# Sixteen of 24 modulation products computed on GpSimd instead of TensorE, in a one-core two-block transformer kernel

## What is computed

```python
c_act = jax.nn.silu(c)
mod = (c_act @ w_ada[l] + b_ada[l])[:, None, :]                  # block 1: 1024 x 6144
sh1, sc1, ga1, sh2, sc2, ga2 = jnp.split(mod, 6, axis=-1)
h = rmsnorm(x, ln1_pre[l]) * (1.0 + sc1) + sh1
proj = h @ w_in[l]                                               # 1024 x 2816
...                                                              # window attention, chunked recurrence (hgrn2)
mix = jnp.concatenate([attn, hg], axis=-1) @ w_out[l]
x = x + ga1 * rmsnorm(mix, ln1_post[l])
...                                                              # 32 experts, then block 2:
mod = (jax.nn.silu(c) @ w_ada + b_ada)[:, None, :]               # 1024 x 6144
mod_ctx = jax.nn.silu(c_ctx) @ w_ada[:, :2 * d] + b_ada[:2 * d]  # the first third, for a second vector
```

## Time and profile before

| | us |
|---|---|
| median of 3 runs | 2185.94 |
| lowest, highest | 2184.53, 2190.42 |
| the profiled execution | 2187.34 |
| its span, first to last instruction | 2185.5 |
| mean granted TensorE clock, of full speed | 0.938 |

### The profile page before, as it was taken

One profiled execution on the slowest core, in us unless ns is written; L12 is line 12 of the kernel. 1 busy time (PEld: TensorE's weight loads), 2 busy tenths in 40 slices (PEclk: granted clock), 3 DMA queues, 4 the chain that ended last, 5 costly groups with the idle time before them and its releaser, 6 DMA issues.

```text
span 2185.5 us, 32417 instructions
## 1 busy us (share of the span) xinstructions
PE 1910.1 (87%) x13222; PEld 1296.8 (59%) x13223; DVE 858.6 (39%) x1997; ACT 551.9 (25%) x1026; POOL 475.8 (22%) x523
## 2 busy tenths in 40 slices
PE   5999998759878279899999989899999999999766
PEld 3777787635433168678766657645565555556432
DVE  3154534353221422521477432334444534443226
ACT  4242512311101431412477412201111211111111
POOL 1000000023221100000345000004444544454320
PEclk9998999879999689979999999889999999999998
DMA  8665521359999451211477322348999999999977
GB/s 323 238 244 178 208 117 58 144 195 413 417 418 397 158 141 53 87 23 55 110 147 168 79 105 88 124 174 340 384 405 358 409 407 376 383 381 399 358 281 307
DMA packets 102472, 527.33 MB, mean 241 GB/s; under 512 B 28002, under 2 KB 28306, under 8 KB 48172
## 3 DMA queue, kind: packets, MB, share of 16 engines
q1 hardware_dynamic: 63216, 451.70, 52.3%
q0 software_dynamic: 36256, 64.54, 10.8%
q10 hardware_dynamic: 2844, 8.85, 1.2%
HBM read 519.36 MB, written 51.90 MB: 261 GB/s over the span
## 4 chain that ended last, share of the span: by engine, by line
PE 71%; DMA 16%; DVE 7%; ACT 3%; issue 2%; SPq 0%; POOL 0%; ACTq 0%; POOLq 0%; DVEq 0%
PE ps L251 31%; PE ps L1738 16%; DMA arena<-in_egu 11%; PE ps L1812 8%; DMA arena<-in_ada 3%; PE ps L1704 2%; PE ps L411 2%; PE ps L2942 1%; PE ps L1799 1%; PE ps L433 1%; PE ps L2968 1%; PE ps L2254 1%; DMA arena<-in_bs_row 1%; PE ps L1073 1%; DMA arena<-y_rows 1%
## 5 line engine op out<-in xcount | busy, mean ns | idle before, releaser
L1738 PE MATMUL ps<-arena 128*64 128x256 f32 x4096 | 484.1, 391 | 63.6 <-DMA arena<-in_egu 52.3
L1738 PEld LDWEIGHTS ps<-arena 128*64 128x64 f32 x4096 | 300.2, 141 | 272.0 <-issue 75.8
L251 PE MATMUL ps<-arena 128*128 128x256 f32 (+4 forms) x1268 | 325.3, 418 | 3.3 <-ACT arena L3092 0.9
L251 PEld LDWEIGHTS ps<-arena 128*128 128x128 f32 (+1 forms) x1268 | 228.0, 204 | 84.1 <-issue 63.6
L1686 POOL DMA_INDIRECT arena<-h_rows,arena x160 | 192.2, 1201 | 297.4 <-DVE arena L1667 133.4
L1692 POOL DMA_INDIRECT y_rows<-arena x160 | 160.5, 1003 | 404.7 <-DVE arena L1843 347.2
L1812 PE MATMUL ps<-arena 128*64 128x512 f32 x1024 | 242.2, 602 | 6.5 <-DVE arena L1807 2.5
L1807 DVE COPY arena<-ps 128x256 f32<-128x256 f32 (+1 forms) x96 | 36.5, 380 | 432.8 <-PE ps L1799 432.8
L1786 ACT ACTIVATE arena<-ps 128x256 f32<-128x256 f32 (+1 forms) x96 | 33.5, 349 | 518.6 <-PE ps L1738 518.6
L2906 POOL DMA_DIRECT2D arena<-in_nabias x160 | 85.5, 542 | 356.9 <-PE ps L2771 200.1
L302 DVE TENSOR_TENSOR wlb<-arena,whb 128x1024 fp32r<-128x1024 f32 (+1 forms) x46 | 55.7, 1212 | 195.7 <-ACT whb L294 195.7
(11 more groups left out here) (429 smaller groups left out, 2776.3 us busy)
## 6 DMA issues: line engine op xcount, KB each, us to landing
arena<-in_egu SPq DMA_DIRECT2D x204, 1024.0 KB, 13.4
arena<-in_ed SPq DMA_DIRECT2D x102, 1024.0 KB, 9.6
arena<-in_ada SPq DMA_DIRECT2D x48, 1024.0 KB, 7.0
arena<-in_win SPq DMA_DIRECT2D x33, 1024.0 KB, 5.1
arena<-y_rows SPq DMA_DIRECT2D x20, 1024.0 KB, 13.7
arena<-in_nabias POOLq DMA_DIRECT2D x96, 128.0 KB, 5.6
arena<-in_wout SPq DMA_DIRECT2D x8, 1024.0 KB, 7.2
h_rows<-arena ACTq DMA_DIRECT2D x8, 512.0 KB, 3.6
```

The costliest lines, as they stand in the source:

```text
L251: z = pe.matmul(o, l, r, start=start and i == 0, stop=stop and i == len(pairs) - 1, skip_group_check=check)
L1738: z = pe.matmul(b[64 * j:64 * j + 64, 256 * s:256 * s + 256], XV[:, c, 64 * h:64 * h + 64], wk(k)[:, j * 256:j * 256 + 256], start=k == 0, ...
```

## The change

For the products in `ON_POOL` (4 to 11 and 16 to 23) GpSimd multiplies the loaded weights, 128 x 2048 words, in their slot by the vector (one word per partition and row block), then adds the eight blocks of 256 columns in halves: 1024, 512 and at last 256 results, the last into the row buffer `MS[n % 2]`. The slot is free after that. TensorE's fold then only sums over all partitions, with a matrix of ones in place of `SEL`. Products 0 to 3 and 12 to 15 stay on TensorE. All folds move: fold n - 2 now stands where product n stood. VectorE's bias additions move with them.

```diff
--- before.py
+++ after.py
@@ -411,10 +411,8 @@
                     z = pe.matmul(b.ap[q:q + 32, i * 256:(i + 1) * 256], CW[layer][:, k, :], wv[:, k, :],
                                   start=k < 4, stop=k >= 4, tile_position=(0, q))
                 z.then_inc(*ada.up("pe", "mm", n, i))
-            if n not in (0, 2, 4):
-                pe_ada_fold(pe, w, n - 1, order)
-            if n in (1, 3, 23):
-                pe_ada_fold(pe, w, n, order)
+
+        ON_POOL = [n for n in range(4, 24) if not 12 <= n < 16]
 
         def act_ada(act, w, n):
             w.wait_ge(*ada.to("mm", n, 1))
@@ -422,16 +420,33 @@
                 w.wait_ge(*ada.to("fold", n - 2))
             act.activation(MS[n % 2], banks.of(ada, "mm", n).ap, ACT.Copy).then_inc(*ada.up("act", "ms", n))
 
+        def pool_ada(pool, w, n):
+            layer = PAIRS[n][0]
+            w.wait_ge(*ada.to("c", layer))
+            w.wait_ge(*ada.to("fold", n - 2))
+            for i in range(2):
+                s = ring.of(ada, "w", n, i)
+                wv, acc = cut(s.ap, 8), MS[n % 2][:, 256 * i:256 * i + 256]
+                w.wait_ge(*s.landed)
+                c = MC1.unsqueeze(2) if layer == 0 else mc2v[:, :, 0:1]
+                pool.tensor_tensor(wv, wv, bc(c, [128, 8, 256]), ALU.mult).then_inc(*ada.up("pool", "part", n, i, 8))
+                for k in (4, 2):
+                    w.wait_ge(*ada.to("part", n, i, 2 * k))
+                    pool.tensor_tensor(wv[:, 0:k, :], wv[:, 0:k, :], wv[:, k:2 * k, :], ALU.add).then_inc(*ada.up("pool", "part", n, i, k))
+                w.wait_ge(*ada.to("part", n, i, 2))
+                pool.tensor_tensor(acc, wv[:, 0, :], wv[:, 1, :], ALU.add).then_inc(*ada.up("pool", "mm", n, i))
+
         def pe_ada_fold(pe, w, n, order=None):
 
             width = ADA[PAIRS[n][0]][3]
             b = banks.turn(ada, ("fold", n), ("mod", n), order)
             for f in b.free:
                 w.wait_ge(*f)
-            w.wait_ge(*ada.to("ms", n))
+            w.wait_ge(*(ada.to("mm", n, 1) if n in ON_POOL else ada.to("ms", n)))
+            w.wait_ge(*ld.to(*ROWS))
             for c in range(4):
-                z = pe.matmul(b.ap[:, c * width:(c + 1) * width], MS[n % 2][:, c * 128:(c + 1) * 128], SEL[:, 0:width],
-                              start=True, stop=True)
+                z = pe.matmul(b.ap[:, c * width:(c + 1) * width], MS[n % 2][:, c * 128:(c + 1) * 128],
+                              ones[:, 0:width] if n in ON_POOL else SEL[:, 0:width], start=True, stop=True)
             z.then_inc(*ada.up("pe", "fold", n))
 
         def dve_ada(dve, w, n):
@@ -649,12 +664,17 @@
             first, turns = [6, 7], [0, 1, 2, 3, 4, 5]
             for n in range(2):
                 pe_ada(pe, w, n, first)
+                if n:
+                    pe_ada_fold(pe, w, 0, first)
+                    pe_ada_fold(pe, w, 1, first)
             w.wait_ge(*ld.to(*VECS))
             for k in range(8):
                 w.wait_ge(*n1.to("xn", 3))
                 pe_turn(pe, w, n1, "n", k, lambda t: scr3[:, t, k * 128:(k + 1) * 128], ("full", k), 4, order=turns)
             for n in (2, 3):
                 pe_ada(pe, w, n, first)
+            for n in (2, 3):
+                pe_ada_fold(pe, w, n, first)
 
         def act_start(act, w):
             act_first(act, w)
@@ -718,8 +738,10 @@
                         for h in (0, 1) if p == 8 else (2, 3):
                             pe_head(pe, w, h)
                     n = ada_of(p, q)
-                    if n:
-                        pe_ada(pe, w, n, KVB if (p, q) == (9, 1) else AB)
+                    if n and n not in ON_POOL:
+                        pe_ada(pe, w, n, AB)
+                    if p:
+                        pe_ada_fold(pe, w, 2 + 2 * p + q, KVB if p == 10 or (p, q) == (9, 1) else AB)
                     if p in (4, 5, 6) and q == 0:
                         pe_pv1(pe, w, p - 4)
                     elif (p, q) == (6, 1):
@@ -892,21 +914,21 @@
                             dve_attn_norm(dve, w)
                             dve_diag(dve, w, wo, "g1", 0, 2, GA)
                         else:
-                            dve_ada(dve, w, 21)
+                            dve_ada(dve, w, 20)
                             for m in range(4):
                                 dve_step(dve, w, m)
                     elif (p, q) == (9, 1):
-                        for k in (22, 23):
-                            dve_ada(dve, w, k)
+                        dve_ada(dve, w, 21)
                         for m in range(4, 8):
                             dve_step(dve, w, m)
                     elif p == 10:
+                        dve_ada(dve, w, 22 + q)
                         for m in range(8, 12) if q == 0 else range(12, 16):
                             dve_step(dve, w, m)
                             if m in (8, 13):
                                 dve_gate1(dve, w, m // 13)
-                    if p < 9 and n > 4:
-                        dve_ada(dve, w, n - 1)
+                    if 0 < p < 9:
+                        dve_ada(dve, w, n - 2)
             for t in range(4):
                 if t == 2:
                     dve_hg_last(dve, w)
@@ -3498,6 +3520,8 @@
             w = Waits(pool)
             pool_first(pool, w)
             pool_rows1(pool, w)
+            for n in ON_POOL:
+                pool_ada(pool, w, n)
             pool_xa(pool, w)
             pool_spill(pool, w)
             pool_na(pool, w)
```

## The result

The changed kernel takes 2289.0 us (median of 4 runs, 2280.6 to 2290.7) against 2185.2 us for the kernel before (4 runs): a ratio of 1.047, 95% interval 1.043 to 1.050, 104 us slower. Forecast: 2281 us. The profiled execution has a span of 2286.5 us, 101.0 longer than before.

What follows compares the result with a forecast made beforehand. GpSimd, holding each of two load slots for 9.6 us, was taken to bound the kernel's stretch from 47 to 327 us: 32 x 9.6 - 212.3 = +95 us on 2185.9, 2281 us, range 2225 to 2350 us.

Steps and rivals of the forecast that it cites:

- What bounds the stretch: 47 to 327 us: two slots carry all modulation loads; GpSimd's time per slot exceeds today's 6.1 us, so GpSimd becomes bound.
- C: Time for which GpSimd holds one slot, its four operations in series: 9.6 us, between 4.0 and 13.5.
- the quiet price: GpSimd's time per slot without VectorE's conflict: 8.3 us for 3840 results plus starts and waits, 9.0 us.
- The conflict: VectorE working in the same memory holds GpSimd up: 0.6 us a slot, between 0 and 2.8.
- Product 12: TensorE's first product after GpSimd's products 4 to 11: done at 58.1 + 16C instead of 139.4, a delay of 72 us.
- The middle: Products 12 to 15 on TensorE: the 55.8 us from product 12's end to product 16's start remain, only shifted.
- the clock: TensorE half idle may run at 1.2 GHz: a few us on top at the stretch's ends, within the range.
- The second stretch: Products 16 to 23: GpSimd needs 16C = 154 us, TensorE at most 132; the state step follows 0.6 us after GpSimd.
- Rival 3: Conflict with VectorE throughout, each waiting for the other: C near 13, +204 us, 2390 us; chance 6%.
- The sum: Delay of the state step behind fold 23: 32C - 212.3, +95 us with C = 9.6.
- The signs: Profile marks: 2048-result operation 4.4 to 4.8 us, TensorE waiting over 100 us for GpSimd; wrong if under 3.5 us.
- Nothing absorbed later: Behind 327 us all is in series and expert loads come equally late, so the 95 us remain in full.

Runs made afterwards that it cites:

- half the change alone: Changed kernel with only products 4 to 11 on GpSimd, 12 to 23 on TensorE: 2248.0 us, ratio 1.030.
- the short hold: Changed kernel without GpSimd's adds of 1024 and 512 results, so products are incomplete: 2204.7 us, a single execution on other values.
- the idle multiplications alone: Kernel before plus sixteen rounds of unused GpSimd multiplications in unused memory, from about 186 us: 2213.7 us, ratio 1.015.
- the write-only run: Changed kernel with GpSimd's four operations a slot replaced by six MEMSETs, modulation vectors zero: 2220.3 us, ratio 1.016, total not to be compared.
- two write-only runs: Changed kernel with MEMSETs for GpSimd's operations, 2220.3 us; kernel before with idle GpSimd MEMSETs of 1024 elements, 2188.8 us.

## Why the prediction came out right, and where it did so by luck

- **What bounds the stretch**: right for GpSimd. Two slots in turn make its time per slot the pace of the first stretch; half the change alone and the short hold show it. But the loads on the chain before, 15.8%, were read as waits that could be won back (up to 44 us); TensorE waited 4.1 us for them.
- **C**: the quiet price was put at 9.0 us, measured 8.1. The multiplication with a repeated operand is the term that was mis-sized: 3.60 us for 2048 results, 1.76 ns each, near my figure for two reads in series (1.73); the adds of two real operands are near the 2.17 I took for all (2.35 us for 1024, 1.26 for 512: 2.13 ns for each further result). The conflict was put at 0.6 us a slot; 8.94 - 8.1 = 0.8 in the first stretch. In all 8.94 against 9.6. On the figure of the Trainium skill ("GPSIMD Engine Reference", section 3.1), C would have been an estimated 9.3, nearer than mine and still high.
- **Product 12**: forecast 212, measured 196.95: 10.6 us from C, 3 from GpSimd's start (46.99, not 50), 1.2 from a quicker load.
- **The middle**: I said it would be shifted unchanged, 55.8 us. It took 62.0 (196.95 to 258.92). Two runs of matmuls of L251 took 10.41 and 12.51 us for 7.40 and 9.43, at a clock of 0.71 (197 to 211 us) and 0.76 (226 to 240) on average. That is 6.1 of the 6.2 us; smaller differences of both signs cancel. The first run stands right behind the wait. Ahead of the second TensorE had been busy for most of 30 us, so that one is not shown to come from the wait. I had named the clock and left it in the range.
- **The second stretch**: the failed step. "All that stands ahead of it on TensorE is done while it waits" is wrong, since VectorE's work was not done. GpSimd's sixteen slots took 155.1 us, near the 153.6 of the sum (with 5.4 us in it in which GpSimd waited for a fold), but the step behind fold 23 came 12.4 us after them, not 0.6. The conflict had been charged to GpSimd alone, at 0.6 us a slot. It fell mostly on VectorE: 123 us busy where it had 61. Behind product 12 the changed kernel loses 42.1 us, the idle multiplications alone, without holding a slot, 28.3, and the write-only run, which holds the slots, 22.0. The two losses overlap, and how they share the 42.1 us was not taken apart.
- **Rival 3** named this conflict and the rule for it, and was dismissed with the words that it matters only in the middle stretch, where GpSimd idles. It matters wherever VectorE is near the chain, which it is from piece 7 on. Its reason against the conflict, that most of VectorE's work in the second stretch reads one operand from PSUM, was a misreading: by the operands' names 21 of the 61 us do (L1094, L889, L443, L1023 and the copies), and with GpSimd beside it the rest went from 40 to 101 us. What the price of 2390 us had wrong is that each would wait for the other all the time: GpSimd lost 0.8 us a slot in the first stretch and 1.3 in the second, not 4.
- **The sum**: the step was to start 94.9 us later and started 99.7 later: -14.8 (product 12), +6.2 (middle), +1.5 and +11.8 (second stretch). Errors of both signs nearly cancelled. That is luck; by the total alone the prediction looks better than it was.
- **The signs**: the multiplication at 3.60 us is under the forecast 4.4 to 4.8 and just above the 3.5 named as a sign of being wrong. "GpSimd named as the releaser, over 100 us in sum" did not come: before the folds TensorE waited 20.9 us with GpSimd named, beside 21.3 us for the loads of product 12 and 62.2 for VectorE in three lines (L977 18.6, L903 25.5, L474 18.1). The first of these three stood behind projection weights that the load queue issued only at 135.99 us, so it is the slots' doing; the other two are the step that failed.
- **Nothing absorbed later**: right. From the step to the end 1860.0 us, 1858.7 before.

## What to carry to other kernels

An idle GpSimd is not free. Before work is given to it, look at what VectorE does in the same stretch and whether that is on the chain: each of its instructions that reads two operands from SBUF, or copies or scales within SBUF, can wait for one whole GpSimd instruction, so long GpSimd instructions beside many short ones of VectorE are the worst case here. Instructions a quarter as long cost a third in these runs. And when an engine takes over work whose input buffers pass through a short ring, its time per buffer, not the time spared on the other engine, sets the pace, also for the loads that stand behind in the same queue.

## What the runs showed of the hardware

- GpSimd, float32, 128 partitions: multiply by a repeated operand 3.60 us for 2048 results; adds 2.35 us for 1024, 1.26 for 512, and 0.72 for 256; MEMSET 1.81 us for 2048. Whether the repeated operand or the multiplication makes a result cheaper than in the adds was not tried.
- VectorE beside it: while GpSimd reads and writes, a tensor_tensor of 512 elements went from 0.69 to 2.8 us beside instructions of up to 3.6 us, to 2.1 beside ones of up to 2.2 us, and to 1.1 beside ones of 0.73 us. The scan (L856) went from 1.21 to 2.70 us. While GpSimd only wrote, tensor_tensor and the scan kept 0.69 and 1.21 us, but tensor_scalar of 128 elements within SBUF went from 0.28 to 1.73 us. Instructions with one operand in PSUM, such as the state steps' (L1094, 343 ns in both kernels), were untouched. The Trainium skill ("SBUF — State Buffer", "Who interferes with whom") says the same: two SBUF inputs contend with a GpSimd instruction that reads, the two-port modes of copy and tensor_scalar with any, and the loser waits for the whole instruction. These runs agree, with one group that needs more than the rule: L869, a product of two SBUF operands, kept 0.68 us wherever GpSimd read, and had 0.86 and 0.79 in the two write-only runs. It stands right behind a copy that was held; why it gets through was not tried.
- The blocking goes both ways: GpSimd's multiplication took 3.60 us alone and up to 4.60 beside VectorE in the changed kernel.
- A wait of TensorE can be paid for twice: in the wait for product 12, from 186 to 197 us, TensorE was busy 3.9 of 11 us and the granted clock was 0.50 (1.2 GHz). The matmuls behind it ran at that level until 205 us (0.63 us for one of 512 columns, 0.39 from then on).
